# Experts' row stores cut into transfers of 6 partitions, and the final norm's weights loaded in another place, in a two-layer hybrid encoder

## What is computed

```
for l in range(2):
    hn = rms_norm(h, attn_norm[l])
    p  = hn @ w_in[l]                      # columns for three mixers and three gates
    ys = retention(p), rwkv7(p), latent_attention(p)
    h  = h + (sum_n sigmoid(gate_n) * (ys_n @ w_branch[l, n])) @ w_o[l]
    hn = rms_norm(h, ffn_norm[l])
    if l == 0: h = h + (silu(hn @ wg) * (hn @ wu)) @ wd
    else:      h = h + sum over the token's top 2 of 8 experts of share * swiglu_e(hn)
return rms_norm(h, final_norm)
```

## Time and profile before

| what | value |
|---|---|
| runs of the kernel | 1680.87 us median of 3 (1680.3 to 1682.52) |
| the profiled execution, first to last instruction (span) | 1678.8 us |
| what the median lies above the span | 2.1 us |
| PE busy | 1624.5 us, 97% |
| moved by DMA | 494.14 MB, mean 294 GB/s |

### The profile page before, as it was taken

The page is one execution under the profiler, slowest core; times in us unless marked ns, Lnnn a source line. Parts: engine busy times, 40 slices in busy tenths (PEclk is TensorE's granted clock), DMA queues, the critical chain, the costliest instruction groups (busy, mean ns, idle before and its releaser), DMA issues.

```text
span 1678.8 us, 34618 instructions
## 1 busy us (share of the span) xinstructions
PE 1624.5 (97%) x15590; PEld 1016.0 (61%) x15590; DVE 642.3 (38%) x1037; ACT 444.0 (26%) x652; POOL 171.7 (10%) x172
## 2 busy tenths in 40 slices
PE   8999999999999999999999999989999799999996
PEld 7878777788888877877754436343362434634433
DVE  6668666655555669657532010000100001000012
ACT  5477423454344566423410000000000000000001
POOL 1264002200000075100400000000000000000010
PEclk9999999999999999999999999999999999999998
DMA  9645213555445743212799999999999999999996
GB/s 347 234 146 201 86 63 118 212 203 186 171 170 201 225 175 110 101 52 101 306 425 429 428 430 428 429 429 429 429 428 427 429 429 429 428 428 420 406 427 256
DMA packets 84250, 494.14 MB, mean 294 GB/s; under 512 B 5528, under 2 KB 14612, under 8 KB 60632
## 3 DMA queue, kind: packets, MB, share of 16 engines
q1 hardware_dynamic: 79360, 480.52, 71.0%
q0 software_dynamic: 2064, 7.67, 1.2%
q10 hardware_dynamic: 2680, 3.74, 0.7%
HBM read 484.78 MB, written 6.16 MB: 292 GB/s over the span
## 4 chain that ended last, share of the span: by engine, by line
PE 81%; DMA 10%; DVE 6%; ACT 2%; issue 1%; SPq 0%; DVEq 0%; ACTq 0%
PE bank L1427 30%; PE bank L2073 26%; PE bank L2092 11%; DMA slot<-moe_units_dram 9%; PE bank L1642 3%; PE bank L1613 2%; PE bank L1419 2%; PE bank L2035 1%; PE bank L2007 1%; DVE ring_lo L2136 1%; DVE tmp L2136 0%; DMA ring<-w_in_dram 0%; PE bank L1997 0%; DVE xterm L2136 0%; DVE xc L2489 0%
## 5 line engine op out<-in xcount | busy, mean ns | idle before, releaser
L2073 PE MATMUL bank<-slot,xg 128*32 128x512 f32 (+1 forms) x5120 | 489.3, 539 | 8.9 <-DMA slot<-moe_units_dram 8.2
L2073 PEld LDWEIGHTS bank<-slot,xg 128*32 128x32 f32 x5120 | 168.5, 110 | 314.4 <-issue 278.7
L2092 PE MATMUL bank<-slot,ehT 128*32 128x256 f32 x4480 | 250.6, 381 | 25.3 <-DMA slot<-moe_units_dram 24.4
L2092 PEld LDWEIGHTS bank<-slot,ehT 128*32 128x32 f32 x4480 | 143.0, 110 | 127.7 <-DMA slot<-moe_units_dram 33.4
L2136 DVE TENSOR_TENSOR ehm<-bank,esg 128x512 f32<-128x512 f32 (+3 forms) x32 | 23.7, 741 | 463.6 <-ACT esg L1329 463.6
L1329 ACT ACTIVATE esg<-bank 128x512 f32<-128x512 f32 (+3 forms) x32 | 20.4, 637 | 491.9 <-PE bank L2073 491.9
L1427 PE MATMUL bank<-i_hi,ix_hi 128*128 128x512 f32 (+2 forms) x288 | 108.4, 376 | 2.0 <-DVE ix_lo L2136 1.0
L1427 PE MATMUL bank<-i_hi,ix_lo 128*128 128x512 f32 (+2 forms) x288 | 107.9, 375 | 0.0
L1427 PE MATMUL bank<-ring_lo,ix_hi 128*128 128x512 f32 (+2 forms) x288 | 107.8, 374 | 0.0
L2136 DVE TENSOR_TENSOR ring_lo<-ring,i_hi 128x2048 fp32r<-128x2048 f32 (+2 forms) x36 | 80.4, 2240 | 61.5 <-ACT i_hi L1007 61.5
L2908 DVE COPY ehT<-bank 128x512 f32<-128x512 f32 (+3 forms) x32 | 23.7, 741 | 208.6 <-PE bank L2035 203.0
(11 more groups left out here) (490 smaller groups left out, 2238.4 us busy)
## 6 DMA issues: line engine op xcount, KB each, us to landing
slot<-moe_units_dram SPq DMA_DIRECT2D x166, 2048.0 KB, 29.5
ring<-w_in_dram SPq DMA_DIRECT2D x25, 2048.0 KB, 8.9
ring<-w_branch_dram SPq DMA_DIRECT2D x6, 2048.0 KB, 7.9
ring<-ffn_w_gate_dram SPq DMA_DIRECT2D x5, 2048.0 KB, 7.9
ring<-ffn_w_up_dram SPq DMA_DIRECT2D x5, 2048.0 KB, 7.8
ring<-ffn_w_down_dram SPq DMA_DIRECT2D x5, 2048.0 KB, 7.9
ring<-w_o_dram SPq DMA_DIRECT2D x2, 2048.0 KB, 8.8
ring<-w_o_dram SPq DMA_DIRECT2D x4, 1024.0 KB, 6.2
```

What stands on the lines that cost most here:

```text
L2073: ins = M(psum[GROUP * p:GROUP * p + GROUP, to:to + width], xg[:, x, o:o + GROUP], w[:, c, p, :], start=x == 0 and to % 512 == 0, stop=x = ...
L2092: ins = M(psum[GROUP * p:GROUP * p + GROUP, o:o + 256], ehT[:, x, GROUP * i:GROUP * i + GROUP], w[:, c, p, :], start=x == 0 and o % 512 == ...
```

## The change

Two edits. The stores of p = 2 and p = 3 are made in five transfers each (6, 6, 6, 6 and 8 partitions) instead of one of 32; those of p = 0 and 1 stay. An item's store is then 12 transfers, and the counts that `ey_stored` is compared with follow (192 in the place of 64 for an item). The transfer of `fgain` is started on POOL in layer 1's latent attention, between the copy of the rotary keys and the rounding of the gate panels, with a wait for the read-out of job sR3; its old place and the wait for o11.1 there go.

```diff
+STORE_ROWS = [[(0, GROUP)]] * 2 + [[(0, 6), (6, 12), (12, 18), (18, 24), (24, GROUP)]] * 2
+STORED = 16 * sum(len(parts) for parts in STORE_ROWS)
...
-        eng.wait_ge(s.ey_stored, pair * 128 + (64 * j + 16))
+        eng.wait_ge(s.ey_stored, pair * (2 * STORED) + (STORED * j + 16))
...
                     for p in range(4):
-                        dst = ey_rows[bass.ds(row, rows_), 256 * p:256 * p + 256]
-                        sp.dma_start(dst.rearrange("(g k) n -> k g n", k=GROUP),
-                                     ey[GROUP * p:GROUP * p + GROUP, 0:256 * groups]
-                                     .rearrange("k (g n) -> k g n", n=256)).then_inc(s.ey_stored, 16)
+                        dst = ey_rows[bass.ds(row, rows_), 256 * p:256 * p + 256].rearrange("(g k) n -> k g n", k=GROUP)
+                        for k0, k1 in STORE_ROWS[p]:
+                            src = ey[GROUP * p + k0:GROUP * p + k1, 0:256 * groups]
+                            sp.dma_start(dst[k0:k1], src.rearrange("k (g n) -> k g n", n=256))\
+                                .then_inc(s.ey_stored, 16)
...
                 own.step(G.tensor_copy(mk[:, t, :, 64:96], each(qa[:, t, 384:416], NH)), s.mla_key_ready)
+            if l:
+                read_out(pool, "sR3.1")
+                pool.dma_start(fgain[:], final_norm.partition_broadcast(P)).then_inc(s.fgain_loaded, 16)
             for n in range(4, 16):
...
-        read_out(pool, "o11.1")
-        pool.dma_start(fgain[:], final_norm.partition_broadcast(P)).then_inc(s.fgain_loaded, 16)
         pool.wait_ge(s.pairs_ready, 1)
...
-        pool.wait_ge(s.ey_stored, last_pair * 128 + (64 + 16))
+        pool.wait_ge(s.ey_stored, last_pair * (2 * STORED) + (STORED + 16))
```

## The result

| what | before | after |
|---|---|---|
| median of 9 runs | 1680.61 us (1679.81 to 1682.52) | 1685.43 us (1684.27 to 1686.49) |
| ratio | | 1.0027, 95% interval 1.0018 to 1.0035 |
| profiled execution, span | 1678.8 us | 1684.7 us (its time: 1686.49 us) |

The change costs 4.8 us. The profiled execution after is the slowest of its nine runs, 1.1 us above their median.

A forecast was written before the change was run, and what follows sets the result against it. Work queued on the late DMA engines from 830 us on was taken to bound the kernel; weights -1.2 and stores -2.5 us, SP's issues 0, sum to -3.7: 1680.87 to 1677.2 us, own range 1676.2 to 1678.8, full range 1675.4 to 1681.5.

The forecast's parts named there:

- if none of the six is late, every late engine gains between 1.4 us and 3.0: Stores on the DMA engines: late engines carry fewer rows of p = 2 and 3; 2.5 us taken, lower end 1.4.
- the six: Engines taken to carry the pieces of six partitions, one partition each: +108 KB, +4.1 us, up to 4.5.
- the stores, put at -2.5 us: Cut stores of p = 2 and 3 relieve the late engines, so the end comes 2.5 us sooner.
- the six are among the late: Rival, at the last units: a late engine among the six ends last, +2.9 to +3.3, about 1684.0 us; chance 0.20.
- 12 us at half rate: Wrong-sign at the kernel's end: the half-rate stretch grows from 8.4 us to 12 us or more if six are late.
- The weights' -1.2 us: Final norm's weights: their 512 KB transfer leaves the full stretch at 847.54 us, saving 1.2 us on all engines equally.
- the new place is free: POOL at about 645 us: the 0.58 us issue hides in 1.54 us idle, the traffic where slices stand at 0.
- late and early eight: In the last 8.4 us about half of the sixteen DMA engines have nothing left; the other half still carries units.
- the instruction packets make the eight late: Inferred: 80 packets of 16 KB on q8 go over eight engines, 6.1 us, the larger part of the 8.4.
- SP's block: Rival: slow store issues hold up the next units, thin stores run dry, about 1684 us; chance 0.07.
- The longer issue for few partitions: Stores on SP: each of ten issues may cost 0.27 us more; block 8.3 us, +6.4, hidden by the queue, cost 0.
- The sign named for this rival: Dips in the DMA share behind stores would show that SP holds up the units.

The follow-up runs named there:

- +54 KB: Changed kernel with only p = 3 cut into 6, 6, 6, 6, 8 and p = 2 one transfer again: 1682.60 us, ratio 1.0012 to the kernel before.
- pieces of 8: Changed kernel with the stores of p = 2 and 3 cut 8, 8, 8, 8: 1683.83 us, ratio 1.0017 to the kernel before.
- 25 and 7: Changed kernel with p = 2 and 3 stored as 25 and 7 partitions: 1677.97 us, ratio 0.9983; with the weights in the old place 1678.28 us.

## Why the prediction was wrong

**The step that failed** is "if none of the six is late, every late engine gains between 1.4 us and 3.0". One of the six, the sixth, is late by these runs: it got 108 KB more, and the stores, put at -2.5 us, cost 4.8. The rival "the six are among the late" held, by its own mechanism: it needed one late engine in the set, the last units, PE's wait for them. Only its sign was another than the one named: not 12 us at half rate, but one engine alone at 0.06. I gave it 0.20, and the lean the other way rested on no row, as the text said. The page "DMA: Bandwidth & Descriptors" of the Trainium skill says, in its section "Why a DMA increments its semaphore by 16 and not by 1", that a transfer from SP takes the largest number of engines up to 16 that divides the slowest dimension, and the lowest-numbered ones. The runs with 5, 6, 7, 8 and 25 partitions agree with the divisor and with sets that lie in one another; which numbers the engines bear no run shows.

**The rival's size.** It was +2.9 to +3.3: rows +4.1 to +4.5, less 1.2 for the weights. The weights gave nothing, so +4.1 to +4.5 is left, against 4.8 measured. Across the runs the loss goes with the sixth engine's rows: +54 KB cost 2.0 us, +72 KB 3.3 us (pieces of 8) and 3.5 (of 7), +108 KB 4.8: 0.037 to 0.049 us a KB, where 26.75 GB/s and the tenth for small packets make 0.038 to 0.042.

**The weights' -1.2 us** failed on "comes off the path". The stretch from 830 to 1550 us was full only because this transfer was in it; without it SP waits for slots, and the 0.50 MB are missing at 864 us. A full share over 720 us does not say that every microsecond of it is needed. That the new place is free was right.

**What bounds the kernel** was right: the late engines set the end, and where they are relieved (25 and 7, or five pieces of 5 and one of 7) it comes 2.7 to 3.2 us earlier. That size is not accounted for. It is near the 2.8 to 3.0 worked out for engines that lose all of p = 2 and 3, but the sixth and the seventh keep one partition of 32 there and should win 1.4 us. The split into late and early eight was right too: evening them out took the half-rate stretch away. That the instruction packets make the eight late was not tried and stays an inference, but the trace before says more for it than the prediction did. From their bytes it took 6.1 us; the earlier trace rows give their time as 0.6% of sixteen engines over 834 us, about 80 us, or 10 us on each of eight, enough for the 8.4. And followed packet by packet in the trace's records from 1641 us on (each packet of an engine starts as the one before it ends), eight engines end their units at 1655 to 1656 us and eight at 1663 to 1665 us, and all three instruction packets of that time lie on the later eight.

**SP's block.** The longer issue for few partitions did not come in the median. Instead single issues took up to 2.9 us and blocks up to 17.58 us, where 6 to 9 were forecast. The sign named for this rival, a dip behind a store, came too: at 1470 us, 0.70 MB in 20 us. That it sets the end is not shown. Five pieces of 5 and one of 7 have 14 issues, a block of 10.17 us at 1466.74 us and the same dip behind it, and are the fastest:

```profile
1478.00:1481.00 3.00, 3.00 (x36) 0.91 (x28) 0.00 (x0) 0.00 (x0) 0.00 (x0) 1.00 0.81 344
```

0.81 is thirteen of sixteen. By the counts above three early engines carry none of the cut rows there, the eighth and two that lie above it; that they are the three that run dry is not shown, but it would be why the dip costs nothing at the end.

**Left out** was that many small transfers in a row can cost more than their bytes: nothing at eight, 5.0 us at twelve on all sixteen engines. Whether that comes from their number on an engine or from SP's longer blocks no run separates. In the change only six engines take twelve. The loss there is at most some tenths above the rows' price, so the two costs do not simply add, and why is open.

## What to carry to other kernels

A transfer spread over few engines moves load between engines, and it pays only if the engines it lands on end early: count the lone engines in the last stretch (a share of 0.06 is one of sixteen) for two or three piece sizes before choosing one. Where the late engines are only known as "half of them", the sign of such an edit is open. And a transfer taken out of a full stretch saves its time only if something else is ready to be moved there: here SP was waiting for slots.

## What was not expected of the hardware

- The late eight are not one half of the order in which transfers take engines: the sixth and seventh are late, the first five and the eighth are not (if transfers of k partitions always take the same first k).
- Eight transfers in a row on every engine cost nothing, twelve cost 5.0 us in 1 KB runs and 5.6 with half of the bytes in 512 B runs, at a DMA share that stays at 1.01: a full share is not a full rate (400 GB/s at 1.02).
- Eight transfers in 512 B runs cost 2.5 us against eight in 1 KB runs' 0, nearly all of it in one dip behind a store.
- With units queued, one store issue on SP took up to 2.9 us and a block of twelve 17.58 us, against 0.3 us for most.
- A transfer of 25 partitions carried its rows as five pieces of 5 do.
